# A two-layer diffusion backbone step: table loads on another queue, a modulation moved into the projection, extra weight slots, a barrier without a drain

## What is computed

```python
def _layer(x, mod, p, lam, lambda_init, rope, ctx_kv):
    sh1, sc1, g1, sh2, sc2, g2 = jnp.split(mod, N_MOD, axis=-1)
    h = _rms(x, p['norm1_g']) * (1.0 + sc1) + sh1
    m, own = _mixing_sublayer(h, p, lam, lambda_init, rope, ctx_kv)
    x = x + g1 * m
    h2 = _rms(x, p['norm2_g']) * (1.0 + sc2) + sh2
    x = x + g2 * _expert_choice_ffn(h2, p['router_w'], p['exp_w_gate'], p['exp_w_up'], p['exp_w_down'])
    return x, own
```

## Time and profile before

| | |
|---|---|
| runs of the kernel | 2136.72 us median (lowest 2130.64) |
| the profiled execution | 2131.46 us |
| its span, first to last instruction | 2129.5 us |
| mean granted TensorE clock | 0.944 of full speed |
| PE busy | 1919.8 us, 90% of the span |
| DVE, ACT, POOL busy | 557.8, 515.2, 456.1 us |
| DMA | 538.38 MB, 253 GB/s over the span |

### The profile page before, as it was taken

The page is one execution under the profiler, slowest core; times in us unless marked ns, Lnnn a source line. Parts: engine busy times, 40 slices in busy tenths (PEclk is TensorE's granted clock), DMA queues, the critical chain, the costliest instruction groups (busy, mean ns, idle before and its releaser), DMA issues.

```text
span 2129.5 us, 40058 instructions
## 1 busy us (share of the span) xinstructions
PE 1919.8 (90%) x17136; PEld 1007.8 (47%) x17136; DVE 557.8 (26%) x1087; ACT 515.2 (24%) x1266; POOL 456.1 (21%) x411
## 2 busy tenths in 40 slices
PE   2999997995999999999959999979859999999993
PEld 1555786452444444444435568844424444444441
DVE  0230777234011010110104147752320101101101
ACT  1111554211221221221212135531112212212221
POOL 0130756000111111111103155620001111111112
PEclk8999998995999999999979999969779999999997
DMA  9400300527999999999970040033449999999995
GB/s 384 172 1 23 143 1 1 218 89 284 360 402 398 396 404 396 395 405 396 403 271 11 0 166 1 1 144 123 163 183 382 404 396 395 404 396 398 402 395 207
DMA packets 146264, 538.38 MB, mean 253 GB/s; under 512 B 8272, under 2 KB 14512, under 8 KB 145936
## 3 DMA queue, kind: packets, MB, share of 16 engines
q1 hardware_dynamic: 123168, 481.87, 57.0%
q0 software_dynamic: 13568, 25.96, 5.0%
q10 hardware_dynamic: 9456, 29.56, 3.7%
HBM read 510.86 MB, written 26.64 MB: 252 GB/s over the span
## 4 chain that ended last, share of the span: by engine, by line
PE 77%; DMA 14%; DVE 4%; SPq 2%; issue 1%; ACT 1%; POOL 1%; POOLq 0%; ACTq 0%; DVEq 0%; PEld 0%
PE PS L659 25%; PE PS L667 13%; DMA ring<-in_exp_w_up 10%; PE PS L549 7%; PE PS L519 5%; PE PS L488 4%; PE PS L455 4%; DMA ring<-in_w_mod 4%; PE PS L424 3%; PE PS L425 3%; PE PS L502 3%; PE PS L426 2%; PE PS L363 1%; PE PS L456 1%; PE PS L489 1%
## 5 line engine op out<-in xcount | busy, mean ns | idle before, releaser
L659 PE MATMUL PS<-ring,arena 128*32 128x512 f32 x6144 | 682.4, 595 | 10.7 <-DMA ring<-in_exp_w_up 5.5
L659 PEld LDWEIGHTS PS<-ring,arena 128*32 128x32 f32 x6144 | 202.3, 110 | 429.8 <-issue 405.1
L667 PE MATMUL PS<-ring,arena 128*32 128x256 f32 x6144 | 349.5, 379 | 0.0
L667 PEld LDWEIGHTS PS<-ring,arena 128*32 128x32 f32 x6144 | 206.0, 110 | 166.5 <-issue 56.6
L1516 POOL DMA_INDIRECT x_rows<-arena x64 | 102.5, 1602 | 639.7 <-DVE arena L1336 589.8
L970 ACT ACTIVATE arena<-PS,modB,modA 128x64 f32<-128x64 f32 x272 | 84.2, 415 | 390.5 <-PE PS L646 390.5
L1502 POOL DMA_INDIRECT arena<-xn_rows,arena x68 | 68.1, 1002 | 351.4 <-DVE arena L1322 268.4
L549 PE MATMUL PS<-ring,H 128*128 128x512 f32 x320 | 140.7, 598 | 1.7 <-ACTq L739 1.7
L1375 POOL TENSOR_SCALAR stat<-stat 128x1 f32<-128x1 f32 (+2 forms) x45 | 13.5, 301 | 537.2 <-ACT arena L937 219.6
L363 PE MATMUL PS<-ring,scT 128*32 128x256 f32 x768 | 63.0, 491 | 57.0 <-DMA ring<-in_w_mod 57.0
L488 PE MATMUL PS<-arena,H 128*128 128x512 f32 x192 | 104.3, 625 | 7.0 <-POOL H L1435 5.8
(11 more groups left out here) (191 smaller groups left out, 1924.6 us busy)
## 6 DMA issues: line engine op xcount, KB each, us to landing
ring<-in_exp_w_gate SPq DMA_DIRECT2D x64, 2048.0 KB, 18.8
ring<-in_exp_w_up SPq DMA_DIRECT2D x64, 2048.0 KB, 20.4
ring<-in_exp_w_down SPq DMA_DIRECT2D x64, 2048.0 KB, 19.9
ring<-in_w_mod SPq DMA_DIRECT2D x24, 2048.0 KB, 12.8
ring<-in_w_in SPq DMA_DIRECT2D x8, 2048.0 KB, 23.9
ring<-in_w_out SPq DMA_DIRECT2D x4, 2048.0 KB, 9.0
arena<-x_rows ACTq DMA_DIRECT2D x15, 512.0 KB, 6.4
x_rows<-arena ACTq DMA_DIRECT2D x10, 512.0 KB, 2.6
```

The lines of the kernel that those rows point to most:

```text
L659: last = mm(PS[64 * c + r:64 * c + r + LANE, bank, :], left[:, c0 + r:c0 + r + LANE], ring[:, s0 + k // 4, k % 4, c * HALF:(c + 1) * HALF] ...
L667: last = mm(PS[32 * j:32 * j + 32, bank, 0:QUART], left[:, c0:c0 + 32], ring[:, s0 + k // 4, k % 4, j * QUART:(j + 1) * QUART], start=(k = ...
```

## The change

Four edits, made together.

1. The five small tables are issued by ACT, behind its first two x tiles, and no longer by SP behind w_in.
2. In layer 1 too SHIFT2 is made inside step j of tile 1 (`FIRST_MODS` of layer 1 is empty).
3. Two more slots, 6 and 7 (`extra`), lie in the last 8192 words of the arena, which phases 4 and 5 don't use. ACT loads them (`load_extra`): GATE2 of the layer at the head of phase 4, and in layer 0 SCALE1 of layer 1, once GATE2's row is taken. PE makes that SCALE1 in phase 4, behind SHIFT1. Pair 2 has three uses fewer over both layers, and the tables of load numbers follow.
4. At the end of phase 5 POOL adds to `phase_done` without a drain.

```diff
+        EXTRA = ARENA - 8 * D
+        extra = arena[:, EXTRA:ARENA].rearrange("p (s k n) -> p s k n", s=2, k=4)
...
         def mod_pair(l, b):
-            return 1 if (l, b) == (0, SCALE1) else {GATE1: 0, SCALE2: 1}.get(b, 2)
+            return {(0, SCALE1): 1, (1, SCALE1): 3}.get((l, b), {GATE1: 0, SCALE2: 1, GATE2: 3}.get(b, 2))
...
-        FIRST_MODS = (((SHIFT1, 2), (SCALE1, 3)), ((SHIFT2, 2),))
+        FIRST_MODS = (((SHIFT1, 2), (SCALE1, 3)), ())
...
                 pair_load(1, w_in_load(l, 1), ins["w_in"], l, D)
-                if l == 0:
-                    for dst, src in ((rope_a[:, :, :, :], ins["k_rope_a"].rearrange("(t p) a n -> p t a n", p=P)),
...
-                        sp.dma_start(dst, src).then_inc(rope_loaded, 16)
                 load_mod(l, SHIFT2)
...
-                load_mod(l, GATE2)
                 if l == 0:
                     load_mod(1, SHIFT1)
-                    load_mod(1, SCALE1)
...
-                    if (l, t) == (0, 1):
-                        modulate(0, SHIFT2, b0 + 2)
+                    if t == 1:
+                        modulate(l, SHIFT2, b0 + 2)
...
                     turn_mod(1, SHIFT1, 3)
+                    modulate(1, SCALE1, 4)
+                    turn_mod(1, SCALE1, 4)
                 wait_apart(pe, k_top, 2 * (l + 1))
...
-                    modulate(1, SCALE1, 4)
-                    turn_mod(1, SCALE1, 4)
                     pe.wait_ge(mod_added, mod_n(1, SCALE1))
...
+            def load_extra(l, b):
+                n = mod_load(l, b)
+                for h in range(2):
+                    if n > 0:
+                        act.wait_ge(slot_used[6 + h], n)
+                    act.dma_start(extra[:, h, :, :], ins["w_mod"][l, h * 512:(h + 1) * 512, b * D:(b + 1) * D]
+                                  .rearrange("(k p) n -> p k n", p=P)).then_inc(slot_ready[6 + h], 16)
...
                 load_xo(l, 1)
+                load_extra(l, GATE2)
...
                 take_mod(l, GATE2, 2)
                 if l == 0:
+                    load_extra(1, SCALE1)
                     take_mod(1, SHIFT1, 3)
+                    take_mod(1, SCALE1, 4)
...
-                finish_phase(l, 5)
+                pool.sem_inc(phase_done, 1)
+                reach(phase_done, 4 * (l * PHASES + 5))
```

More of the change, by code:

```diff
@@ L149, in backbone_step_kernel, with slot @@
         g2b = carve(WIDE)
+        EXTRA = ARENA - 8 * D
+        assert at[0] <= EXTRA, at[0]
+        extra = arena[:, EXTRA:ARENA].rearrange("p (s k n) -> p s k n", s=2, k=4)
+        def slot(s):
+            return ring[:, s, :, :] if s < 6 else extra[:, s - 6, :, :]
         xg = carve(2 * WIDE).rearrange("p (b n) -> p b n", b=2)
@@ L241, in expert_load @@
         def expert_load(l, pair):
-            return ((2, 3, 6), (20, 21, 25))[l][pair]
+            return ((2, 3, 4), (20, 21, 22))[l][pair]
         def mod_load(l, b):
-            return ({SHIFT1: 0, SCALE1: 0, SHIFT2: 1, GATE1: 1, SCALE2: 2, GATE2: 3},
-                    {SHIFT1: 4, SCALE1: 5, SHIFT2: 22, GATE1: 19, SCALE2: 20, GATE2: 24})[l][b]
+            return ({SHIFT1: 0, SCALE1: 0, SHIFT2: 1, GATE1: 1, SCALE2: 2, GATE2: 0},
+                    {SHIFT1: 3, SCALE1: 1, SHIFT2: 20, GATE1: 19, SCALE2: 20, GATE2: 2})[l][b]
         def mod_pair(l, b):
-            return 1 if (l, b) == (0, SCALE1) else {GATE1: 0, SCALE2: 1}.get(b, 2)
+            return {(0, SCALE1): 1, (1, SCALE1): 3}.get((l, b), {GATE1: 0, SCALE2: 1, GATE2: 3}.get(b, 2))
         def w_out_load(l):
-            return (2, 23)[l]
+            return (2, 21)[l]
         MODS = ((0, SHIFT1), (0, SCALE1), (0, SHIFT2), (0, GATE1), (0, SCALE2), (0, GATE2),
                 (1, SHIFT1), (1, SCALE1), (1, SHIFT2), (1, GATE1), (1, SCALE2), (1, GATE2))
-        FIRST_MODS = (((SHIFT1, 2), (SCALE1, 3)), ((SHIFT2, 2),))
+        FIRST_MODS = (((SHIFT1, 2), (SCALE1, 3)), ())
         def mod_n(l, b):
@@ L363, in modulate @@
                             last = mm(PS[32 * q:32 * q + 32, bank, 256:512], scT[:, k, :],
-                                      ring[:, s, kk, q * 256:(q + 1) * 256], start=(k == 0), stop=(k == KD - 1))
+                                      slot(s)[:, kk, q * 256:(q + 1) * 256], start=(k == 0), stop=(k == KD - 1))
                     last.then_inc(slot_used[s], 1)
@@ L411, in step_j @@
                     b0 = 2 + 3 * (t % 2)
[L412 to L415, removed]
-                    if (l, t) == (0, 1):
-                        modulate(0, SHIFT2, b0 + 2)
+                    if (l, t) == (0, 0):
+                        pe.wait_ge(mod_added, mod_n(0, SCALE1))
+                    if t == 3:
+                        pe.wait_ge(mod_added, mod_n(l, SHIFT2))
+                    if t == 1:
+                        modulate(l, SHIFT2, b0 + 2)
                     for k in range(KD):
@@ L1146, in _ @@
                         step_q(l, n)
-                        if (l, n) == (0, 1):
-                            add_mod(0, SHIFT2, 7)
+                        if n == 1:
+                            add_mod(l, SHIFT2, 7)
                         if n == 4:
```

26 lines of the change are left out of this document (13 added, 13 removed).

## The result

The changed kernel takes 2116.74 us in the median (2116.01 to 2119.72), beside 2134.08 of the kernel before on the same chip: a ratio of 0.9926, interval 0.9909 to 0.9942. The ratio leaves out one of the four runs of the kernel before, which took 2514.14 us. The gain is clear of the runs' scatter, and under 2%. The forecast was 2114.0 with a range of 2104 to 2126. The profiled execution has a span of 2114.7 us, 14.8 less than the 2129.5 before; the sum of the terms was 17.6.

A forecast was written before the change was run, and what follows sets the result against it. The prediction took the expert loops as full (PE busy 523.10 of 526 us in the first) and their lengths as fixed. Terms -8.5 + 3.3 - 7.0 - 5.4 = -17.6 took 2131.5 to 2114 us, range 2104 to 2126.

The forecast's parts named there:

- The start, -8.5: Start of layer 0: with the tables ahead of w_in, j0 starts at 49.2 instead of 58.3; 8.5 us gained.
- Rival C: Start: j0 waits for both halves of w_in, gain only 4.0 us, total 2118.5; chance 0.08.
- The idle stretch "in either case": Before j0: TensorE comes from idleness before and after, now with less run-up, so 8.5 was taken instead of 9.1.
- The top-k, +3.3: Layer 0's top-k: SCALE1 lands late, first expert starts 0.8 us later and its first matmuls run colder; 3.3 us lost.
- the colder first expert: Head of layer 0's expert loop: first 64 matmuls take 9.76 us, not 7.07; 2.7 more, less a little.
- SCALE1's landing: Layer 0's top-k: SCALE1, sharing the DMA engines with expert 0's down weights, lands at about 520 us.
- The half share: Layer 0's top-k: SCALE1 and the down weights, loading together, each get half of 410 GB/s.
- Rival A: Layer 0's top-k: SCALE1 lands at 512, before the top-k ends; term -4.5, total 2106 us; chance 0.20.
- From layer 0 to layer 1, -7.0: Layer turn: without drain and SHIFT2 wait j0 comes 11.5 us earlier; SHIFT2's modulation costs some back; net 7.0 gained.
- The end, -5.4: Kernel end: without GpSimd's drain the five final x loads come earlier; 5.4 us gained.
- Rival B: Barriers: what the drain waited for still holds GpSimd or the x loads; total 2124.5 us; chance 0.08.
- Rival D: Expert loops: the weight stream loses its lead, every expert takes 33.50 us; +20.2, total 2134; chance 0.04.

The follow-up runs named there:

- e3: Changed kernel with the five table loads back on SyncE's queue behind w_in; 2124.36 us.
- e4: Kernel before with the tables, SHIFT2 and barrier edits but without the extra slots; 2116.59 us.
- e6: Changed kernel with one more wait on SyncE, issuing layer 0's expert 0 down weights only after the first gather landed; 2110.64 us.
- e1: Changed kernel with GpSimd's drain put back at the end of both expert loops; 2127.13 us.
- e2: Changed kernel with layer 1's SHIFT2 made ahead of the projection again; 2123.22 us.
- e11: Repeat of the changed kernel with layer 0's expert 0 down weights held until the first gather landed; 2109.38 us.

## Why the prediction was right, point by point

The forecast was right in its sign and in most of its terms. That the sums meet so well is in part luck. By the stages of the first profile, the four places gave -7.9, +1.25, -6.9 and -4.1, together -17.7 where -17.6 stood, since a loss at the top-k that was 2.05 too large in the forecast made up for 0.6 at the start and 1.3 at the end. The second profile of the same kernel gives -6.6, +2.25, -5.8 and -4.2, together -14.3. The first profile's way from -17.7 to -14.8 is 3.6 lost by phase 3's clock, which no term foresaw, less 0.8 gained in the phases before it.

1. **The start, -8.5.** The reading of the chain held: j0 is released by the later of the two first halves of w_in, at 49.44 for 49.2. That load is issued at 30.31 where it was 28.4 and again takes 19.0, so the tables ahead of it cost 1.9 for the 1.8 worked out. Rival C, both halves, falls with it. The idle stretch "in either case" is in the rows too (20.30 us and 1.94 of transposes before, 7.73 and nothing now), but its price was too small: the 0.6 allowed were 0.7 to 2.4. And the step that a gain at the start is carried to phase 4 whole did not hold; e3 shows 1.2 to 5.6 us of it there, and where it is least (e4), the clock in phase 3 takes about half of the rest.
2. **The top-k, +3.3.** Measured +1.25 (-1.27 to the first expert, +2.52 in the loop), and +2.25 in the second profile; e4 puts it at 0.3 to 2.6. Of the sum, the colder first expert was about right (8.38 and 9.89 for the first 64 matmuls where 9.76 stood, against 7.07), and so was the short gather (3.2 for 2.98). The term mis-sized is SCALE1's landing: worked out for 520, which is 515.0 when phase 4 starts 5.05 earlier, and measured 513.25. The half share was right (1.64 MB each from 502 to 510 us). What was too small is the stretch that SCALE1 has for itself: 0.94 MB were allowed for it, and 1.57 MB went through alone from 496 to 500 us. The direction, a second queue is no second road, is what e6 shows: 13.0 us against 19.15. Rival A falls.
3. **From layer 0 to layer 1, -7.0.** Measured -6.9, by the steps of the prediction: the x loads at 1072.1 less the 3.8 by which the loop ends earlier is 1068.3 (1068.26 in the trace), j0 at 1083.7 (1083.89). The cold TensorE, allowed 1.0, cost 1.15 (5.57 from tile 0's transposes to j0, for 4.42). e1 and e2 take the two edits back one at a time and find j0 5.65 and 8.75 later behind the loop's end. In the second profile the turn gave -5.8.
4. **The end, -5.4.** Measured -4.1. The x loads come 5.6 earlier behind the loop; 1.4 of it is lost behind the last store, which the prediction did not see. Rival B falls with e1.

Rival D, the weight stream's lead: in the chain of the changed kernel the up weights of late experts are waited for from 846.92 on. But the loop is only 2.5 longer (4.2 in the second profile, most of it the first expert's cold matmuls), and e6, counted from phase 4, starts it 5.6 earlier and ends it 6.0 earlier although expert 0's down weights come later, so no stream set its end. The loss that D feared is not there.

## What to carry to other kernels

A second issuing queue gave a load here another place in the order, and half of the DMA engines once SyncE's load flowed beside it: put what is waited for first alone on the DMA engines and hold back what is wanted later (one wait on SyncE was worth about 6 us here, where the extra slots by themselves were worth nothing). Where several waits end close together, as SHIFT2 and the x tiles behind the drain did, ask of each edit what is late next: two edits can pay more together (6.9 us here) than the sum of what each pays alone (0.7 and 3.1). And when a stage changes its length, read the granted clock before looking for a wait.

## What had not been expected of the hardware

- TensorE's clock after a wait of 2.31 us in phase 3 is either level in profiles of one and the same program: 35.8 or 32.2 us for the phase. Five matmuls of no use in that wait (2.32 us) went with the full level in both layers of the one profile taken, but so did e11's profile without them.
- The place of a loop in an engine's instructions can cost more than all edits here together: 336 more instructions ahead of it brought stalls of 5.6 to 6.2 us at every turn of the loop, 113 instead of 48 packets on the instruction queue, and 56 to 58 us in that loop.
- A GpSimd drain that takes 5.46 us ahead of the final loads costs 4.0 us at the end of the kernel (e1), since without it 1.4 more pass behind the last store.
